# Order of the latent up projections and place of the modulation products in a two-block transformer kernel

## The chip, the cores and the metric

One Trainium2 chip (trn2), one core of it. The metric is the device time of one execution in microseconds (us). The kernel before was run three times: median 2625.8 us, from 2625.59 to 2627.35. One further execution was taken with the hardware profiler; all rows below are from that one.

## The reference, cut to what matters

Two blocks of two layers each run on a sequence of 512 tokens with 1024 features, all in float32. The change is in the first block only, in its token mixer, once per layer:

```python
mod = jax.nn.silu(c) @ w_ada[l] + b_ada[l]                 # 6 x 1024, the modulation
sh1, sc1, g1, sh2, sc2, g2 = jnp.split(mod[:, None, :], 6, axis=-1)
h = x * (1.0 + sc1) + sh1
proj = h @ w_in                                            # qa ka va iq ik iw cq ckv kr ga gb
...
# index scores of the sparse attention: sum over 8 heads of relu(iq . ik) * iw, top 128 kept
q  = (rms_norm(cq, q_norm_g) @ w_uq).reshape(bsz, seq, 8, 64 + 32)    # latent up, queries
q_nope, q_rope = q[..., :64], apply_rope(q[..., 64:], positions)
kv = (rms_norm(ckv, kv_norm_g) @ w_ukv).reshape(bsz, seq, 8, 64 + 64) # latent up, keys and values
```

Both versions compute all of it. The modulation of layer l is needed late: sh1 and sc1 first, g1 and part of sc2/sh2 by the end of the layer.

## The kernel before, in words

The program is written engine by engine with explicit semaphores; nothing schedules it. Each engine's list is in order, and a wait holds everything behind it on that engine.

**Weights.** Every weight slot is 128 x 2048 float32 (the slot of the key/value up projection, UKV, is 128 x 1024). SyncE loads it to w_raw (two buffers, L436), ScalarE rounds it to w_hi (`split_hi`, L1212), GpSimd forms w_lo = w_raw - w_hi (L550), and TensorE computes each product as three matmuls of 512 columns, hi x hi, lo x hi and hi x lo (`mm3`, L623 to L625). The slots of a layer follow each other: 0 to 3 the input projection for the index heads and latents, 4 to 7 the gate ga, 8 the query up projection (UQ), 9 UKV, 10 and 11 the first ones of the dense queries and keys (QK).

**Modulation.** Each layer's w_ada arrives in halves of 512 outputs, each as two loads (ring `ada_mid`, L430; a load waits until the one two before it is consumed). VectorE multiplies and adds it up in eight steps of 128 x 512, 4 per load: in a plain loop (`ada_halves`, L1686 and L1688), or one step at a time between other work (`ada_step_at`, L1702 and L1708). TensorE then sums over the partitions with matmuls of one column each (`ada_group`, L655); a float32 matmul is two passes, so 20 of them are 40 weight loads and 40 short matmuls. `ada_take` (L1714, L1717) adds the bias.

**The stretch of the change, per layer.** While TensorE runs the input projection, VectorE works through halves 4, 5 and 6 of the layer in the loop, and behind them in its list forms iw_tok (L1942), for which TensorE waits before the index scores. Index scores: 12 pairs of heads and query blocks (`PAIRS`); per pair TensorE has two score products (L867), then 5 or 6 of the 64 gate steps; ScalarE takes the relu (L1386), VectorE adds up (L1956, L1959). The banks of a pair are free again when VectorE has added up the pair two before. Between them stand two reciprocals of the latent norms (L1968, L1971) and 16 modulation steps of halves 7 and 8.

Latent up stage: 8 query tiles of 6 matmuls (two k-steps), then 4 key tiles of 3, then 4 value tiles of 3, through banks 0 to 3 in turn; after query tile 3 stand all 20 one-column products, in bank 7. For a query tile VectorE makes two rope products (L1989, L1990), then ScalarE copies the rest and frees the bank (L1409) and GpSimd adds the two (L586); VectorE writes the products of head h only after GpSimd has added those of head h-2. For a key tile ScalarE copies both heads (L1415, L1416). Value tiles are copied by VectorE (L1997), in order and after all key tiles are free. ScalarE splits slot 10 between the query tiles and the key tiles, and slot 11 after the last value tile. Then `attention(l, 1)` begins: TensorE's score product (L730) and three gate-like steps of slot 10 per unit beside it, which need w_lo of slot 10 and the bank of value tile 2.

## Time and profile before

| | before |
|---|---|
| median of 3 runs | 2625.8 us (2625.59 to 2627.35) |
| the profiled execution's own time | 2619.64 us |
| its span (first to last instruction) | 2617.9 us |
| time around the span | 1.7 us |
| TensorE busy | 2454.3 us, 94% |
| VectorE, ScalarE, GpSimd busy | 1195.2, 1022.6, 960.6 us |
| mean granted TensorE clock | 0.968 of full |
| index scores and up stage, layer 0 | about 99 to 191 us of the span |
| the same, layer 1 | about 954 to 1042 us |

In the timeline a row is: start, duration, engine, line, operation, out<-in, count, and in brackets the idle time before it with what ended it. PEld is TensorE's weight load, PE its matmul. Busy PE is not PE at its peak: a matmul of 512 columns is shown as 0.39 us long, though the next starts after 0.23 us. In the windows, PEclk is the granted clock as a share of the full 2.4 GHz.

### The profile page before, as it was taken

What the parts mean: (1) busy time and instruction counts of PE and PEld (TensorE: products, weight loads), DVE (VectorE), ACT (ScalarE), POOL (GpSimd) and SP (SyncE); (2) the same over time, 40 slices, a digit from 0 to 9 for tenths busy, and PEclk for the clock granted to TensorE, in tenths of its full rate; (3) what the DMA queues carried; (4) which work ended last, traced back from release to release, by engine and by line L of the source; (5) the groups of instructions that cost most, each with busy time, mean ns of one, the idle gap of its engine ahead of it and who ended that gap; (6) DMA issues with size and microseconds to landing.
All of it is one profiled execution on the core that took longest, in us unless ns stands there. A gap on an engine that the chain in (4) does not pass through costs nothing.

```text
span 2617.9 us, 32182 instructions
## 1 busy us (share of the span) xinstructions
PE 2454.3 (94%) x11316; PEld 1906.0 (73%) x11316; DVE 1195.2 (46%) x2581; ACT 1022.6 (39%) x1679; POOL 960.6 (37%) x780
## 2 busy tenths in 40 slices
PE   7999999899999899999989999989999989899877
PEld 4668767688888776876767888857788767577555
DVE  7555665654453465566555444134200530544562
ACT  6344344244442244434424444132223432323652
POOL 2342223434444434222344444443444434244211
PEclk9999999999999899999999999999999999899878
DMA  9521133222235342113322222222222202122100
GB/s 342 198 91 65 62 97 143 101 81 96 96 133 182 119 173 102 65 62 97 135 110 80 96 96 87 100 81 83 85 96 96 86 33 80 49 93 84 49 1 33
DMA packets 51985, 259.12 MB, mean 99 GB/s; under 512 B 6368, under 2 KB 16352, under 8 KB 26272
## 3 DMA queue, kind: packets, MB, share of 16 engines
q1 hardware_dynamic: 50720, 249.24, 27.4%
q0 software_dynamic: 1152, 8.39, 0.8%
q8 instruction: 69, 1.13, 0.2%
q14 instruction: 44, 0.36, 0.0%
HBM read 249.08 MB, written 7.34 MB: 98 GB/s over the span
## 4 chain that ended last, share of the span: by engine, by line
PE 87%; DVE 6%; ACT 3%; issue 3%; POOL 1%; DMA 1%; SPq 0%; DVEq 0%; ACTq 0%; POOLq 0%
PE bank L623 24%; PE bank L625 23%; PE bank L624 23%; PE bank L730 3%; PE bank L754 2%; PE bank L743 1%; PE bank L1069 1%; PE bank L998 1%; PE bank L1142 1%; PE bank L867 1%; PE bank L1161 1%; PE bank L655 1%; POOL w_lo L550 1%; PE bank L1058 1%; ACT w_hi L1212 1%
## 5 line engine op out<-in xcount | busy, mean ns | idle before, releaser
L550 POOL TENSOR_TENSOR w_lo<-w_raw,w_hi 128x512 fp32r<-128x512 f32 (+1 forms) x700 | 887.5, 1299 | 1444.1 <-ACT w_hi L1212 898.7
L623 PE MATMUL bank<-h_hi,w_hi 128*128 128x512 f32 x1792 | 735.8, 411 | 33.3 <-DVE h_lo L2083 14.3
L625 PE MATMUL bank<-h_hi,w_lo 128*128 128x512 f32 x1792 | 705.1, 393 | 0.0
L624 PE MATMUL bank<-h_lo,w_hi 128*128 128x512 f32 x1792 | 704.0, 393 | 0.0
L623 PEld LDWEIGHTS bank<-h_hi,w_hi 128*128 128x128 f32 x1792 | 341.0, 190 | 130.4 <-issue 62.2
L624 PEld LDWEIGHTS bank<-h_lo,w_hi 128*128 128x128 f32 x1792 | 341.0, 190 | 73.0 <-issue 8.4
L625 PEld LDWEIGHTS bank<-h_hi,w_lo 128*128 128x128 f32 x1792 | 339.6, 190 | 73.7
L1212 ACT ACTIVATE w_hi<-w_raw 128x2048 fp32r<-128x2048 f32 (+1 forms) x108 | 189.8, 1757 | 282.6 <-PE bank L625 243.8
L2041 DVE SCALAR_TENSOR_TENSOR cv<-bank,par,cv 128x511 f32<-128x511 f32 (+1 forms) x176 | 131.7, 749 | 215.2 <-ACT cv L1464 202.3
L1464 ACT ACTIVATE cv<-bank,par 128x512 f32<-128x512 f32 x88 | 68.3, 779 | 234.9 <-PE bank L625 234.9
L1217 ACT ACTIVATE w_hi<-w_raw 128x2048 fp32r<-128x2048 f32 x76 | 145.0, 1909 | 35.9 <-PE bank L625 35.9
L1288 ACT ACTIVATE L<-L,nmax 128x128 f32<-128x128 f32 (+3 forms) x128 | 72.0, 563 | 186.9 <-DVE nmax L1769 186.4
L623 PE MATMUL bank<-u_hi,w_hi 128*128 128x512 f32 x352 | 138.7, 394 | 0.0
L625 PE MATMUL bank<-u_hi,w_lo 128*128 128x512 f32 x352 | 137.7, 391 | 0.0
L624 PE MATMUL bank<-u_lo,w_hi 128*128 128x512 f32 x352 | 137.6, 391 | 0.0
L623 PE MATMUL bank<-w_hi,h_hi 128*128 128x512 f32 x256 | 100.8, 394 | 0.0
L625 PE MATMUL bank<-w_hi,h_lo 128*128 128x512 f32 x256 | 99.7, 389 | 0.0
L624 PE MATMUL bank<-w_lo,h_hi 128*128 128x512 f32 x256 | 99.6, 389 | 0.0
L1850 DVE SCALAR_TENSOR_TENSOR x<-bank,mod,x 128x512 f32<-128x512 f32 x32 | 24.0, 751 | 159.6 <-PE bank L625 158.6
L2121 DVE TENSOR_TENSOR wt<-bank,decay 128x512 f32<-128x512 f32 (+3 forms) x32 | 13.5, 484 | 172.0 <-PE bank L1058 171.8
L2092 DVE TENSOR_TENSOR rt<-bank,rope 128x512 f32<-128x512 f32 x32 | 22.1, 691 | 126.7 <-PE bank L998 112.5
L624 PEld LDWEIGHTS bank<-u_lo,w_hi 128*128 128x128 f32 x352 | 66.5, 189 | 14.3 <-issue 0.5
(345 smaller groups left out, 3669.3 us busy)
## 6 DMA issues: line engine op xcount, KB each, us to landing
w_raw<-w_stream SPq DMA_DIRECT2D x150, 1024.0 KB, 4.8
w_raw<-w_down SPq DMA_DIRECT2D x32, 704.0 KB, 4.1
ada_mid<-w_ada SPq DMA_DIRECT2D x20, 1024.0 KB, 6.9
ada_last<-w_ada SPq DMA_DIRECT2D x12, 1024.0 KB, 4.8
ada_early<-w_ada POOLq DMA_DIRECT2D x8, 1024.0 KB, 19.5
ada_late<-w_ada SPq DMA_DIRECT2D x8, 1024.0 KB, 6.2
bias_in<-bias_scratch SPq DMA_DIRECT2D x16, 256.0 KB, 3.1
bias_in<-bias_scratch SPq DMA_DIRECT2D x16, 192.0 KB, 2.7
```

The lines of the kernel that those rows point to most:

```text
L550: ins = nc.gpsimd.tensor_tensor(w_lo[r][:, part], w_raw[r][:, part], w_hi[r][:, part].bitcast(fp32), ALU.subtract)
L623: nc.tensor.matmul(out, w[0][:, cols], xh, start=first, stop=False)
L624: nc.tensor.matmul(out, w[0][:, cols], xl, start=False, stop=False)
L625: return nc.tensor.matmul(out, w[1][:, cols], xh, start=False, stop=last)
L655: ins = nc.tensor.matmul(banks[bank][:, j:j + 1], ada_acc[late][:, part + j // 4, (j % 4) * P:(j % 4 + 1) * P], ones[:, 0:1], start=True, ...
L730: nc.tensor.matmul(banks[4 + t % 2][:, 0:n], q[rows, hh, i * P:(i + 1) * P], kk[rows, hh, 0:n], start=True, stop=True).then_inc(s_done, 1)
L754: ins = nc.tensor.matmul(banks[u % 2][:, 0:HD], PT[u % 2][:, b * P:(b + 1) * P], v[:, b, h * HD:(h + 1) * HD], start=(b == 0), stop=(b == i))
L1212: A_(w_hi[n % 2][:, 0:cols], w_raw[n % 2][:, 0:cols], ACT.Copy).then_inc(w_hi_done, 1)
L1217: A_(w_hi[n % 2][:, :], w_raw[n % 2][:, :], ACT.Copy).then_inc(w_hi_done, 1)
L1288: A_(L[t % 3][:, 0:n], L[t % 3][:, 0:n], ACT.Exp, bias=nmax[:, t:t + 1], scale=-1.0, accum_out=esum[:, t:t + 1]).then_inc(exp_done, 1)
L1464: A_(cv[s][c][:, :], banks[(t + c) % 4][:, :], ACT.Identity, bias=b, scale=w2).then_inc(conv_first, 1)
L2041: return V.scalar_tensor_tensor(out, banks[(t + c) % 4][:, 0:S - 2 + w], weight, out, ALU.mult, ALU.add)
```

## The change

A table `UPS` puts the key tiles between the query tiles: q0 q1 q2 k0 q3 q4 k1 q5 q6 k2 q7 k3, on TensorE and ScalarE alike; VectorE keeps its order of heads. The 20 one-column products are issued in twos, after each of the tiles at positions 4 to 11 and after value tiles 0 and 1. The modulation half 6 leaves the loop ahead of iw_tok and joins halves 7 and 8 inside the index scores, two steps per pair. The wait of pair 1 for the loop, and the place of `ada_take`, move with it.

```diff
--- before.py
+++ after.py
@@ -411,6 +411,8 @@
         def ended(kind, u):
             return next((t for t, k in BESIDE[kind][u] if k == BESIDE_LAST[kind]), None) if 0 <= u < len(BESIDE[kind]) else None
 
+        UPS = [("q", 0), ("q", 1), ("q", 2), ("k", 0), ("q", 3), ("q", 4), ("k", 1), ("q", 5), ("q", 6), ("k", 2), ("q", 7),
+               ("k", 3)]
         LOADS = 16 * 3
         BIAS_UNITS = [(i, 8 * i + q) for i in range(NB) for q in range(8)]
         BIAS_BANKS = (2, 3, 6, 7)
@@ -648,6 +650,12 @@
                         if after_slot:
                             after_slot(it, s)
 
+            def ada_columns_at(first, count):
+                for j in range(first, first + count):
+                    ins = nc.tensor.matmul(banks[7][:, j:j + 1], ada_acc[0][:, j // 4, (j % 4) * P:(j % 4 + 1) * P],
+                                           ones[:, 0:1], start=True, stop=True)
+                return ins
+
             def ada_group(first, halves, late, bank):
                 pe.wait_ge(ada_used, 2 * (first + halves))
                 part = first % 12 - 4 if first % 12 else 0
@@ -861,7 +869,7 @@
                     if u >= 2:
                         pe.wait_ge(idx_acc, NI * l + 2 * (u - 1))
                     if u == 1:
-                        pe.wait_ge(ada_used, 2 * (12 * l + 7))
+                        pe.wait_ge(ada_used, 2 * (12 * l + 6))
                     for c in range(2):
                         rows = slice(c * HD, (c + 1) * HD)
                         nc.tensor.matmul(banks[4 + 2 * (u % 2) + c][:, 0:n], iq[rows, p, i * P:(i + 1) * P], ik2[rows, 0:n],
@@ -883,24 +891,28 @@
 
                 pe.wait_ge(c_done, 3 * (l + 1))
                 w = split(l, SLOT_UQ)
+                wkv = split(l, SLOT_UKV)
                 wait_slot(l, SLOT_UQ)
-                for h in range(H):
-                    wait_bank(l, TILE_UQ + h, 2 if h < 2 else 4)
-                    if h == 3:
+                for pos, (what, j) in enumerate(UPS):
+                    wait_bank(l, TILE_UQ + pos, 2 if pos < 2 else 4)
+                    if pos == 3:
                         pe.wait_ge(ada_used, 2 * (12 * l + 9))
-                    tile(banks[h % 4][:, :], w, h * 2 * P, c_hi, c_lo, 2).then_inc(tile_done, 1)
-                    if h == 3:
                         pe.wait_ge(idx_acc, NI * (l + 1))
-                        ada_group(12 * l + 4, 5, 0, 7)
-                w = split(l, SLOT_UKV)
-                wait_slot(l, SLOT_UKV)
-                for j in range(4):
-                    wait_bank(l, TILE_UK + j)
-                    tile(banks[j][:, :], w, j * P, c_hi, c_lo, 1, 2).then_inc(tile_done, 1)
+                        wait_slot(l, SLOT_UKV)
+                    if what == "q":
+                        tile(banks[pos % 4][:, :], w, j * 2 * P, c_hi, c_lo, 2).then_inc(tile_done, 1)
+                    else:
+                        tile(banks[pos % 4][:, :], wkv, j * P, c_hi, c_lo, 1, 2).then_inc(tile_done, 1)
+                    if pos >= 4:
+                        ada_columns_at(2 * pos - 8, 2)
                 for m in range(NB):
                     wait_bank(l, TILE_UV + m)
                     mm3(banks[m][:, :], (c_hi[:, 2, m * P:(m + 1) * P], c_lo[:, 2, m * P:(m + 1) * P]), slice(0, P),
-                        w[0][:, 512:1024], w[1][:, 512:1024], True, True).then_inc(tile_done, 1)
+                        wkv[0][:, 512:1024], wkv[1][:, 512:1024], True, True).then_inc(tile_done, 1)
+                    if m < 2:
+                        ins = ada_columns_at(16 + 2 * m, 2)
+                        if m:
+                            ins.then_inc(ada_sum, 1)
                 attention(l, 1)
 
                 A = aidx(l, 1)
@@ -1403,17 +1415,20 @@
                         m = SLOT_GA + tt // 2 + 2
                         split_hi(l, m, 1024 if m == SLOT_UKV else SLOT)
 
-                for h in range(H):
-                    act.wait_ge(tile_done, tdone(l, TILE_UQ + h))
-                    act.wait_ge(q_rope, H * l + h + 1)
-                    A_(qm[0:64, h, :], banks[h % 4][0:64, :], ACT.Copy).then_inc(tile_evac, 1)
-                split_hi(l, SLOT_UQ + 2)
-                act.wait_ge(ada_used, 2 * (12 * l + 9))
                 act.wait_ge(kr_turned, l + 1)
-                for j in range(4):
-                    act.wait_ge(tile_done, tdone(l, TILE_UK + j))
-                    A_(km[0:64, 2 * j, :], banks[j][0:64, :], ACT.Copy)
-                    A_(km[0:64, 2 * j + 1, :], banks[j][64:128, :], ACT.Copy).then_inc(tile_evac, 1)
+                for pos, (what, j) in enumerate(UPS):
+                    b = banks[pos % 4]
+                    act.wait_ge(tile_done, tdone(l, TILE_UQ + pos))
+                    if what == "q":
+                        act.wait_ge(q_rope, H * l + j + 1)
+                        A_(qm[0:64, j, :], b[0:64, :], ACT.Copy).then_inc(tile_evac, 1)
+                        if j == H - 1:
+                            split_hi(l, SLOT_UQ + 2)
+                    else:
+                        if j == 0:
+                            act.wait_ge(ada_used, 2 * (12 * l + 9))
+                        A_(km[0:64, 2 * j, :], b[0:64, :], ACT.Copy)
+                        A_(km[0:64, 2 * j + 1, :], b[64:128, :], ACT.Copy).then_inc(tile_evac, 1)
                 act.wait_ge(tile_done, tdone(l, TILE_UV + 3))
                 split_hi(l, SLOT_UKV + 2)
                 softmax(l, 1)
@@ -1937,7 +1952,7 @@
                     dve.wait_ge(rope_ready, 1)
                     chain(V.tensor_scalar(rope[64:128, S:2 * S], rope[64:128, S:2 * S], ck[64:128, C_SGN:C_SGN + 1], None,
                                           ALU.mult))
-                ada_halves(12 * l + 5, 2, 0, 1, 7)
+                ada_halves(12 * l + 5, 1, 0, 1, 7)
                 dve.wait_ge(iw_done, l + 1)
                 V.tensor_scalar(iw_tok[:, :], banks[4][:, 0:32], H ** -0.5, None, ALU.mult).then_inc(iw_ready, 1)
                 dve.wait_ge(iw_ready, l + 1)
@@ -1978,23 +1993,24 @@
                             dve.wait_ge(c_hid, 3 * l + j + 1)
                             V.tensor_tensor(c_lo[:, j, :], c_raw[:, j, :], f32(c_hi[:, j, :]), ALU.subtract
                                             ).then_inc(c_done, 1)
-                    for e in range(16 * u // len(PAIRS), 16 * (u + 1) // len(PAIRS)):
-                        ada_step_at(12 * l + 7 + e // 8, 3 + e // 8, e % 8 // 4, e % 4)
+                    for e in range(2 * u, 2 * u + 2):
+                        ada_step_at(12 * l + 6 + e // 8, 2 + e // 8, e % 8 // 4, e % 4)
                 dve.wait_ge(idx_acc, NI * (l + 1))
 
                 for h in range(H):
-                    dve.wait_ge(tile_done, tdone(l, TILE_UQ + h))
+                    pos = UPS.index(("q", h))
+                    b = banks[pos % 4]
+                    dve.wait_ge(tile_done, tdone(l, TILE_UQ + pos))
                     if h >= 2:
                         dve.wait_ge(q_sum, H * l + h - 1)
-                    V.tensor_tensor(q_cos[h % 2][64:96, :], banks[h % 4][64:96, :], rope[64:96, 0:S], ALU.mult)
-                    V.tensor_tensor(q_sin[h % 2][64:96, :], banks[h % 4][96:128, :], rope[96:128, S:2 * S], ALU.mult
+                    V.tensor_tensor(q_cos[h % 2][64:96, :], b[64:96, :], rope[64:96, 0:S], ALU.mult)
+                    V.tensor_tensor(q_sin[h % 2][64:96, :], b[96:128, :], rope[96:128, S:2 * S], ALU.mult
                                     ).then_inc(q_rope, 1)
-                    if h == 5:
-                        ada_take(l, 1)
                 for m in range(NB):
                     dve.wait_ge(tile_done, tdone(l, TILE_UV + m))
                     dve.wait_ge(tile_evac, tdone(l, TILE_UV + m - 1))
                     V.tensor_copy(vm[:, m, :], banks[m][:, :]).then_inc(tile_evac, 1)
+                ada_take(l, 1)
                 softmax(l, 1)
                 topk_loop(2, TOPK // 8 + 1 - AHEAD)
                 topk_step(2, TOPK // 8)
```

On TensorE, in the up stage of layer 0 (c_hi and c_lo are the normed latents, w_hi_52 is the UQ slot, w_hi_53 the UKV slot, ada_acc_early the summed modulation), before:

```order
L623 MATMUL bank<-c_hi,w_hi_52 128x512
L624 MATMUL bank<-c_lo,w_hi_52 128x512
L625 MATMUL bank<-c_hi,w_lo_54 128x512
L655 MATMUL bank<-ck,ada_acc_early 128x1 x20
L623 MATMUL bank<-c_hi,w_hi_52 128x512
```

and now, from the middle of it:

```order
L655 MATMUL bank<-ck,ada_acc_early 128x1 x2
L625 MATMUL bank<-c_hi,w_hi_53 128x512
L626 MATMUL bank<-c_lo,w_hi_53 128x512
L627 MATMUL bank<-c_hi,w_lo_55 128x512
L655 MATMUL bank<-ck,ada_acc_early 128x1 x2
L625 MATMUL bank<-c_hi,w_hi_52 128x512
```

The block of 20 has become ten groups of two, and a key tile (w_hi_53) stands between query tiles.

On ScalarE, in the same stage (qm and km are the query and key outputs; w_hi_52<-w_raw_50 is the split of slot 10, the last row that of slot 11), before:

```order
L1212 ACTIVATE w_hi_53<-w_raw_51 128x1024
L1409 ACTIVATE qm<-bank 64x512 x8
L1212 ACTIVATE w_hi_52<-w_raw_50 128x2048
L1415 ACTIVATE km<-bank 64x512
L1416 ACTIVATE km<-bank 64x512
...
L1212 ACTIVATE w_hi_53<-w_raw_51 128x2048
```

and now:

```order
L1224 ACTIVATE w_hi_53<-w_raw_51 128x1024
L1424 ACTIVATE qm<-bank 64x512 x3
L1430 ACTIVATE km<-bank 64x512
L1431 ACTIVATE km<-bank 64x512
L1424 ACTIVATE qm<-bank 64x512 x2
...
L1424 ACTIVATE qm<-bank 64x512
L1224 ACTIVATE w_hi_52<-w_raw_50 128x2048
L1430 ACTIVATE km<-bank 64x512
L1431 ACTIVATE km<-bank 64x512
L1224 ACTIVATE w_hi_53<-w_raw_51 128x2048
```

Three of the four key tiles are now copied ahead of the split of slot 10, which still follows the last query tile.

On VectorE, from the loop into the index scores of layer 0, now (before, the loop ran three times in all, and the 16 steps were spread one or two to a pair):

```order
L1703 SCALAR_TENSOR_TENSOR bank<-ada_mid_144,csilu,bank 128x512 x3
L1703 SCALAR_TENSOR_TENSOR ada_acc_early<-ada_mid_144,csilu,bank 128x512
L1692 REGISTER_ALU
L1692 COMPARE_AND_BRANCH
L1957 TENSOR_SCALAR iw_tok<-bank 128x32
L1971 TENSOR_SCALAR sel<-bank,iw_tok 128x256
L1974 SCALAR_TENSOR_TENSOR sel<-bank,iw_tok,sel 128x256
L1717 TENSOR_SCALAR bank<-ada_mid_143,csilu 128x512
L1723 SCALAR_TENSOR_TENSOR bank<-ada_mid_143,csilu,bank 128x512
L1974 SCALAR_TENSOR_TENSOR sel<-bank,iw_tok,sel 128x256 x2
```

iw_tok now follows one pass of the loop, and every pair is followed by two steps.

## Rows read from the trace of the kernel before

**Rows 1.** The page: the span, and the engines of the chain that ended last.
```profile
span 2617.9 us, 32182 instructions
...
PE 87%; DVE 6%; ACT 3%; issue 3%; POOL 1%; DMA 1%; SPq 0%; DVEq 0%; ACTq 0%; POOLq 0%
```

**Rows 2.** Timeline, layer 0, from the input projection into the index scores.
```profile
88.11 0.33 SPq L430 DMA_DIRECT2D ada_mid<-w_ada  x1
...
95.74 2.34 DVE L1688 SCALAR_TENSOR_TENSOR bank<-ada_mid,csilu,bank 128x512 f32<-128x512 f32 x3 [2.79 <-DMA ada_mid<-w_ada]
...
96.01 0.39 PE L625 MATMUL bank<-h_hi,w_lo 128*128 128x512 f32 x1
...
99.46 0.33 PEld L867 LDWEIGHTS bank<-ik,iq 64*128 64x128 f32 x4 [3.48 <-issue]
...
102.01 0.63 PE L625 MATMUL bank<-h_hi,w_lo 128*128 128x512 f32 x1
...
107.05 0.30 PEld L867 LDWEIGHTS bank<-ik,iq 64*128 64x128 f32 x4 [0.76 <-issue]
```

**Rows 3.** Timeline, layer 1, the same place: pairs 0 and 1.
```profile
953.54 0.33 PEld L867 LDWEIGHTS bank<-ik,iq 64*128 64x128 f32 x4 [1.83 <-issue]
...
959.59 0.30 PEld L867 LDWEIGHTS bank<-ik,iq 64*128 64x128 f32 x4 [0.76 <-issue]
```

**Rows 4.** Timeline, layer 0, pairs 5 and 6, and VectorE's dearest work between.
```profile
125.86 0.30 PEld L867 LDWEIGHTS bank<-ik,iq 64*128 64x128 f32 x4 [0.35 <-issue]
...
128.57 3.34 DVE L1971 RECIPROCAL c_sq<-c_sq 128x512 f32<-128x512 f32 x1
...
131.02 0.30 PEld L867 LDWEIGHTS bank<-ik,iq 64*128 64x128 f32 x4 [0.35 <-issue]
...
133.94 0.75 DVE L1708 SCALAR_TENSOR_TENSOR bank<-ada_mid,csilu,bank 128x512 f32<-128x512 f32 x1
```

**Rows 5.** Timeline, layer 0, the latent up stage.
```profile
159.84 0.19 PEld L623 LDWEIGHTS bank<-c_hi,w_hi 128*128 128x128 f32 x1
...
161.70 0.69 DVE L1989 TENSOR_TENSOR L<-bank,rope 32x512 f32<-32x512 f32 x1 [2.09 <-PE bank L625]
...
161.89 2.54 POOL L550 TENSOR_TENSOR w_lo<-w_raw,w_hi 128x512 fp32r<-128x512 f32 x2 [6.45 <-ACT w_hi L1212]
...
165.28 5.56 PEld L655 LDWEIGHTS bank<-ck,ada_acc_early 128*128 128x128 f32 x40
...
170.73 0.33 PEld L623 LDWEIGHTS bank<-c_hi,w_hi 128*128 128x128 f32 x1
...
181.86 0.59 ACT L1409 ACTIVATE qm<-bank 64x512 f32<-64x512 f32 x1 [0.84 <-DVE O L1990]
...
182.35 1.90 ACT L1212 ACTIVATE w_hi<-w_raw 128x2048 fp32r<-128x2048 f32 x1
...
184.33 4.97 POOL L550 TENSOR_TENSOR w_lo<-w_raw,w_hi 128x512 fp32r<-128x512 f32 x4 [1.22 <-ACT w_hi L1212]
...
189.11 3.08 DVE L1997 COPY vm<-bank 128x512 f32<-128x512 f32 x4 [7.34 <-ACT km L1416]
...
191.50 0.19 PEld L623 LDWEIGHTS bank<-h_hi,w_hi 128*128 128x128 f32 x1 [1.25 <-issue]
```

**Rows 6.** Timeline, layer 1, start, one-column products and end of that stage.
```profile
1012.38 0.19 PEld L623 LDWEIGHTS bank<-c_hi,w_hi 128*128 128x128 f32 x1
...
1017.82 4.84 PEld L655 LDWEIGHTS bank<-ck,ada_acc_early 128*128 128x128 f32 x40
...
1022.54 0.34 PEld L623 LDWEIGHTS bank<-c_hi,w_hi 128*128 128x128 f32 x1
...
1042.45 0.19 PEld L623 LDWEIGHTS bank<-h_hi,w_hi 128*128 128x128 f32 x1 [1.45 <-issue]
```

**Rows 7.** Windows: stretch, length, busy and count per engine, PEclk, DMA share, GB/s.
```profile
165.30:170.70 5.40, 5.40 (x42) 5.36 (x40) 2.77 (x4) 1.18 (x2) 4.23 (x4) 0.83 0.65 207
170.70:177.00 6.30, 6.30 (x19) 5.03 (x19) 2.25 (x4) 0.59 (x1) 1.27 (x1) 0.60 0.00 0
```

## The prediction, made before the changed kernel ran

> **What bounds the kernel.** The first view is the chain of waits: 87% of the span is TensorE's own work [rows 1], so time is won where TensorE waits or runs slow. The second view is the timeline of the two places that the diff touches, read backwards from the row at which TensorE goes on; the third is the granted clock by window. They show three losses in each layer.
>
> First, before the index scores. TensorE's last matmul of the input projection starts at 96.01, and the first score product loads at 99.46, after 3.48 us without a load. In between VectorE ends the modulation loop (the load issued at 88.11 is first used at 95.74, and four steps follow), and iw_tok stands behind it [rows 2]. In layer 1 the gap is 1.83 [rows 3]. A score product with nothing to wait for has a gap of 0.35 [rows 4], so 3.13 and 1.48 us are the loop's.
>
> Second, the clock behind that gap. In layer 0 a matmul at 102.01 lasts 0.63 instead of 0.39 us: 1.2 GHz. Pair 0 to pair 1 takes 107.05 - 99.46 = 7.59 us [rows 2], and in layer 1, at 2.4 GHz, 959.59 - 953.54 = 6.05 [rows 3]. A fall of the clock so costs 1.54 us.
>
> Third, the up stage. It lasts from 159.84 to 191.50, 31.66 us [rows 5], and from 1012.38 to 1042.45, 30.07 us [rows 6], counted to the load of the first step beside the attention. TensorE has far less to do in it: 72 matmuls at 0.227 (24 take 165.28 - 159.84 = 5.44) and 40 short passes. The 40 take 1022.54 - 1017.82 = 4.72 us in layer 1, 0.118 each [rows 6], and 5.45 in layer 0 [rows 5]; together 21.1 us. The rest is low clock after the block of one-column products (0.60 of full over 6.3 us [rows 7], a loss of 2.5 us), and a tail in which TensorE waits for ScalarE: slot 10 is split at 182.35 for 1.90 us, only then are eight key halves copied at 0.6 us each, and VectorE's value copies begin at 189.11 [rows 5].
>
> **Part 1, the moved modulation half.** Eight steps of 0.75 us [rows 4] leave the loop; with one half less it ends near 88.1, since the row of its next load, issued when half 5 is consumed, stands there [rows 2]. iw_tok is then some ten us early, and TensorE goes on at 96.33: minus 3.13 and minus 1.48. Without the gap the clock has no reason to fall in layer 0: minus 1.54. The eight steps, 6.2 us with their gaps, now stand among the pairs. Pair 5 takes TensorE 131.02 - 125.86 = 5.2 us, and it is VectorE's worst: the reciprocal of 3.34, two steps of 0.75, and two additions and three products that are each no longer than a step [rows 4], some 8.3 us. It falls behind by some 3 us and catches up over pairs 6 and 7; TensorE waits only for the additions of the pair two before, which leaves about 3 us to spare. I cost it at nothing; if that cover were gone, each us of lag beyond it is a us of TensorE. SyncE: the loads of half 7 now wait for half 6 inside the pairs, and the weight loads of slots 7 to 9 queue behind them. By my count slot 7 is issued at 109 instead of 104 and split at about 128; the modulation load issued with it is needed 11 us later and the slowest seen took 95.74 - 88.11 = 7.6 us [rows 2]. Nothing is late.
>
> **Part 2, the up stage.** Time t runs from the stage's first load; everything before it is shifted as a whole.
> - q0 to q2 end at 4.08. k0 needs w_lo of UKV, whose row ends 161.89 + 2.54 = t 4.59 [rows 5]: a new wait of 0.5 us, k0 ends at 5.33.
> - From there to the end of q7 stand five query tiles (6.80), two key tiles (1.36) and six pairs of columns, 24 passes x 0.118 = 2.83: t = 16.3. The ScalarE and VectorE work of each tile is by then 2 us or more ahead of the bank's next use, since the key copies (1.2 us) fit between query copies (0.59).
> - After q7: 0.50 to VectorE's start (its first row is at t 1.86, the tile ends at 1.36), two products 1.4, ScalarE's copy 0.1 + 0.59: t = 18.9. Split of slot 10, 1.90: 20.8. GpSimd's four parts, 4.97 + 0.1: t = 25.9 [rows 5].
> - k3 is copied after the split, to 22.1, value tile 3 ends at 22.8, the value copies at 25.2. So the **low half of slot 10 is what is late next**: TensorE goes on at t = 26.0. `ada_take` (two small operations) falls before that, and the first transposes stand two units behind it.
>
> The stage then takes 26.0: minus 5.66 in layer 0, minus 4.07 in layer 1. But TensorE is idle from about t 23 to 26. A gap of that length in [rows 2] cost 1.54, and I charge that at the head of the attention in both layers: plus 3.08.
>
> Bounds. How a pair of one-column products prices between wide matmuls is not in these rows. Nearest below: its first load hides, three passes of 0.118; above: one load of 0.19 more is exposed. Over the six pairs on the path that is -0.7 to +1.1 us a layer; I take 0.118 a pass as in the block, because there the loads already paced it. The charge for the clock lies between 0 and 1.54 per layer.
>
> The Trainium skill, "TensorE: Matmul & The Clock Gate", section "Loop structure matters more than you think", has it that matmuls issued back to back keep the engine warm and that a wait between bursts is when the "PE goes cold". The trace disagrees in one place: the clock was 0.83 over 165.3 to 170.7 and 0.60 after it, while the engine was busy 5.40 of 5.40 us [rows 7]; one-column passes alone took it down. By that section the spread columns could not harm the clock and rivals C and E have no chance (2613.0 stands); by the row they could, and 2619.4 is open.
>
> **Sum.** Layer 0: 3.13 + 1.54 + 5.66 - 1.54 = 8.79. Layer 1: 1.48 + 4.07 - 1.54 = 4.01. Together **12.8 us**: span 2617.9 to 2605.1, that execution's 2619.6 to 2606.8. The runs' median stands 6.2 us above the profiled execution, so 2625.8 - 12.8 = **2613.0**. Behind the stage TensorE is busy nearly without a break, so the gain should reach the end.
>
> **Rivals.**
> - **B, the clock holds at the head of the attention** in both layers. For: in layer 1 an idle gap of 1.83 us cost no clock [rows 3]. Against: [rows 2]. Saves 15.9 us: 2609.9. Chance 0.20.
> - **C, the spread columns still bring the clock down once a layer.** For: [rows 7], left after their block. Against: wide matmuls now hold over 60% of the time between. Price as in layer 0 before, 2.5 plus the block's 5.45 - 4.72 = 0.7: 3.2 a layer, 6.4: 2619.4. Chance 0.10.
> - **D, the index scores give the first part back.** VectorE's lag at pair 5, or a modulation load stuck behind a weight slot, makes TensorE wait by 3 to 6 us; or iw_tok was not the last wait, and the change does not do there what it says. For: 8.3 us of work against 5.2. Against: the slack worked out above. At worst the whole 6.15 is lost: 2619.2. Chance 0.09.
> - **E, slower.** The clock falls at position 4 of the up stage and stays at 1.2 GHz until the attention, since each pair of columns comes before it has recovered. The 11.0 us of work from t 5.3 to 16.3 then take twice that, which puts t at 37: plus 5.3 and 6.9, plus 3.1 at the head of the attention, minus 6.1 of part 1: **9 us slower, 2635**. It decides against the change once the low clock covers some 60% of those 11 us in both layers. For: [rows 7]. Against: there the passes stood alone; with six matmuls of 512 columns between, nothing in the rows shows it. Chance 0.04.
> - The forecast keeps 0.57.
>
> **How the numbers follow.** The likeliest case gives 2613.0, with its own range of 2611 to 2616 by the bounds of the columns and half the clock's charge. The range reaches down to B with cheap columns (2609.9 - 1.4 = 2608.5) and up to C and D with dear ones (2620.5); E and the tails are left out. A measurement can tell 0.2%, 5.25 us, from no change. Forecast, B, C and most of D lie beyond it (C and D by a us only, so part of them, 0.06, counts as the same); slower is E, 0.04; faster is 0.90.
>
> **What would show it.** In the changed profile: the load of the first score product at about 96.3 with a gap near 0.35, and at 952.1 in layer 1; clock 1.00 over pair 0; the stage's first load at about 155.2 and 1010.9; k0 waiting for GpSimd's w_lo by half a us; ten groups of x4 short passes at 0.47 us each with wide matmuls at 0.39 between them; the split of slot 10 ended at t 20.8, and the first load beside the attention at t 26.0, released by GpSimd. The prediction is wrong if that load comes after t 28, if a score product waits for `sel`, or if matmuls of 0.63 us appear between the pairs of columns.

## The result, and the profile after

| | before | after |
|---|---|---|
| median of 4 runs | 2625.70 us (2623.18 to 2627.35) | 2609.24 us (2603.87 to 2609.83) |
| ratio, with 95% interval | | 0.9934 [0.9916, 0.9951] |
| the profiled execution | 2619.64 us | 2609.83 us |
| its span | 2617.9 us | 2608.0 us |
| TensorE busy | 2454.3 us | 2452.2 us |
| mean granted clock | 0.968 | 0.968 |

The changed kernel is faster. By the ratio the gain is 0.0066 x 2625.8 = 17 us, with an interval from 13 to 22. By the spans of the two profiled executions it is 9.9 us. The prediction said 12.8 and lies between these two. That one change has two sizes is the main question of the experiments. The two profiles themselves give part of the answer: at the places of the change they differ by 13.7 us (first and sixth row of the table below), and 3.8 us of that is lost elsewhere, 0.9 of it ahead of the first of these places, where the last projection matmul starts at 96.91 instead of 96.01.

The diff adds lines ahead of most helpers, so the old L623 to L625 are L625 to L627 in what follows, the score product's L867 is L875, the attention's L730 is L738, the copies L1409, L1415 and L1416 are L1424, L1430 and L1431, the split L1212 is L1224, GpSimd's L550 is L552. Timeline of after, layer 0, where the index scores begin (beside [rows 2]); a row is start, duration, engine, line, operation, count, and in brackets the idle time and what ended it:

```profile
88.03 0.75 DVE L1703 SCALAR_TENSOR_TENSOR ada_acc_early<-ada_mid,csilu,bank 128x512 f32<-128x512 f32 x1
88.98 0.19 DVE L1957 TENSOR_SCALAR iw_tok<-bank 128x32 f32<-128x32 f32 x1 [0.20 <-DVE ada_acc_early L1703]
...
96.91 0.39 PE L627 MATMUL bank<-h_hi,w_lo 128*128 128x512 f32 x1
97.22 0.30 PEld L875 LDWEIGHTS bank<-ik,iq 64*128 64x128 f32 x4 [0.35 <-issue]
...
103.22 0.30 PEld L875 LDWEIGHTS bank<-ik,iq 64*128 64x128 f32 x4 [0.76 <-issue]
```

VectorE's loop now starts its last step at 88.03, and iw_tok stands at 88.98, eight us before the last projection matmul at 96.91. The gap of 3.48 us is 0.35, and pair 0 to pair 1 is 103.22 - 97.22 = 6.00 us instead of 7.59. Layer 1 has 0.35 and 951.53 - 945.54 = 5.99:

```profile
945.54 0.30 PEld L875 LDWEIGHTS bank<-ik,iq 64*128 64x128 f32 x4 [0.35 <-issue]
951.53 0.30 PEld L875 LDWEIGHTS bank<-ik,iq 64*128 64x128 f32 x4 [0.76 <-issue]
```

The moved steps cost the index scores nothing. Timeline of after, layer 0, round the reciprocal (beside [rows 4]):

```profile
122.02 0.30 PEld L875 LDWEIGHTS bank<-ik,iq 64*128 64x128 f32 x4 [0.35 <-issue]
...
124.74 3.34 DVE L1986 RECIPROCAL c_sq<-c_sq 128x512 f32<-128x512 f32 x1
...
127.19 0.30 PEld L875 LDWEIGHTS bank<-ik,iq 64*128 64x128 f32 x4 [0.35 <-issue]
...
130.11 1.54 DVE L1723 SCALAR_TENSOR_TENSOR bank<-ada_mid,csilu,bank 128x512 f32<-128x512 f32 x2
...
131.68 0.30 PEld L875 LDWEIGHTS bank<-ik,iq 64*128 64x128 f32 x4 [0.35 <-issue]
```

Pair 5's two steps end at 131.65, when pair 7 is about to start (131.68), and still each score load has a gap of 0.35: the lag stays under the slack.

Timeline of after, layer 0, the up stage (beside [rows 5]):

```profile
156.01 0.19 PEld L625 LDWEIGHTS bank<-c_hi,w_hi 128*128 128x128 f32 x1
...
160.71 0.19 PEld L625 LDWEIGHTS bank<-c_hi,w_hi 128*128 128x128 f32 x1 [0.66 <-issue]
...
162.67 0.64 PEld L655 LDWEIGHTS bank<-ck,ada_acc_early 128*128 128x128 f32 x4
163.23 0.19 PEld L625 LDWEIGHTS bank<-c_hi,w_hi 128*128 128x128 f32 x1
...
174.69 1.90 ACT L1224 ACTIVATE w_hi<-w_raw 128x2048 fp32r<-128x2048 f32 x1
...
176.67 9.90 POOL L552 TENSOR_TENSOR w_lo<-w_raw,w_hi 128x512 fp32r<-128x512 f32 x8 [1.21 <-ACT w_hi L1224]
...
177.73 0.19 PEld L625 LDWEIGHTS bank<-w_hi,c_hi 128*128 128x128 f32 x1 [0.92 <-ACT km L1431]
177.78 3.07 DVE L2012 COPY vm<-bank 128x512 f32<-128x512 f32 x4 [3.67 <-ACT km L1431]
...
181.68 0.19 PEld L625 LDWEIGHTS bank<-h_hi,w_hi 128*128 128x128 f32 x1 [2.96 <-POOL w_lo L552]
...
187.86 0.14 PEld L751 LDWEIGHTS bank<-ck,L 128*128 128x128 f32 x1
```

The stage takes 181.68 - 156.01 = 25.67 us, and in layer 1 the same 25.67 (next rows). Ten groups of four short passes stand between the tiles, and 162.67 to 163.23 is 0.56, less the 0.12 by which the next load follows closer: about 0.45 a group over all, or 0.11 a pass, where the block had 0.118. The split of slot 10 starts 18.7 us into the stage, its low half is ready 25.6 us into it, and TensorE waits 2.96 us for it. Layer 1:

```profile
1004.32 0.19 PEld L625 LDWEIGHTS bank<-c_hi,w_hi 128*128 128x128 f32 x1
...
1026.04 0.19 PEld L625 LDWEIGHTS bank<-w_hi,c_hi 128*128 128x128 f32 x1 [0.92 <-ACT km L1431]
...
1029.99 0.29 PEld L625 LDWEIGHTS bank<-h_hi,w_hi 128*128 128x128 f32 x1 [2.95 <-POOL w_lo L552]
```

Windows of after over the columns and tiles, and over the wait with the head of the attention in layer 1 (columns as in [rows 7]):

```profile
165.30:170.70 5.40, 5.40 (x31) 4.62 (x31) 3.36 (x6) 2.80 (x5) 3.50 (x3) 1.00 0.03 14
170.70:177.00 6.30, 6.30 (x39) 5.41 (x37) 1.80 (x3) 4.47 (x6) 2.89 (x3) 1.00 0.00 0
1028.00:1034.60 6.60, 4.61 (x15) 3.77 (x16) 2.67 (x9) 3.07 (x6) 6.60 (x6) 0.74 0.44 159
```

With the columns spread the clock holds (1.00 against 0.83 and 0.60). It falls behind the wait for GpSimd instead: from the first load beside the attention to the first transposes is 6.18 us in layer 0, 187.86 - 181.68, where before it was 4.56.

### The profile page after: what moved, and what is told of

Read it like the earlier page. It is cut to its first block, busy times and chain, and to the rows that moved or that the text cites. A ratio compares the mean times of both kernels' runs of the same rounds, so it can differ in the third digit from the quotient of the medians.

```text
span 2608.0 us, 32138 instructions
## 1 busy us (share of the span) xinstructions
PE 2452.2 (94%) x11316; PEld 1904.3 (73%) x11316; DVE 1193.8 (46%) x2581; ACT 1021.8 (39%) x1679; POOL 960.4 (37%) x780
## 4 chain that ended last, share of the span: by engine, by line
PE 87%; DVE 5%; ACT 3%; issue 2%; POOL 2%; DMA 1%; SPq 0%; DVEq 0%; POOLq 0%; ACTq 0%
PE bank L625 24%; PE bank L627 24%; PE bank L626 23%; PE bank L738 3%; PE bank L762 2%; PE bank L751 1%; POOL w_lo L552 1%; PE bank L1081 1%; PE bank L1010 1%; PE bank L1154 1%; PE bank L875 1%; PE bank L1173 1%; PE bank L1070 1%; PE bank L786 1%; ACT w_hi L1224 0%
## 5 line engine op out<-in xcount | busy, mean ns | idle before, releaser
L552 POOL TENSOR_TENSOR w_lo<-w_raw,w_hi 128x512 fp32r<-128x512 f32 (+1 forms) x700 | 887.3, 1299 | 1439.9 <-ACT w_hi L1224 892.6
L625 PE MATMUL bank<-h_hi,w_hi 128*128 128x512 f32 x1792 | 736.9, 411 | 36.6 <-DVE h_lo L2099 14.3
L627 PE MATMUL bank<-h_hi,w_lo 128*128 128x512 f32 x1792 | 706.1, 394 | 0.0
L625 PEld LDWEIGHTS bank<-h_hi,w_hi 128*128 128x128 f32 x1792 | 341.6, 191 | 134.2 <-issue 59.5
L627 PEld LDWEIGHTS bank<-h_hi,w_lo 128*128 128x128 f32 x1792 | 340.2, 190 | 73.7
L1224 ACT ACTIVATE w_hi<-w_raw 128x2048 fp32r<-128x2048 f32 (+1 forms) x108 | 189.8, 1757 | 281.5 <-PE bank L627 242.4
L625 PE MATMUL bank<-u_hi,w_hi 128*128 128x512 f32 x352 | 138.8, 394 | 0.0
L627 PE MATMUL bank<-u_hi,w_lo 128*128 128x512 f32 x352 | 137.6, 391 | 0.0
L625 PE MATMUL bank<-w_hi,h_hi 128*128 128x512 f32 x256 | 100.8, 394 | 0.0
L627 PE MATMUL bank<-w_hi,h_lo 128*128 128x512 f32 x256 | 99.7, 389 | 0.0
```

Of the source, the lines that this page charges most:

```text
L552: ins = nc.gpsimd.tensor_tensor(w_lo[r][:, part], w_raw[r][:, part], w_hi[r][:, part].bitcast(fp32), ALU.subtract)
L625: nc.tensor.matmul(out, w[0][:, cols], xh, start=first, stop=False)
L627: return nc.tensor.matmul(out, w[1][:, cols], xh, start=False, stop=last)
L1224: A_(w_hi[n % 2][:, 0:cols], w_raw[n % 2][:, 0:cols], ACT.Copy).then_inc(w_hi_done, 1)
```

## The experiments

Five lengths in each layer's trace are compared, and the span: the **gap** from the last projection load to the first score load (0.54 where nothing waits), **pair 0 to 1** (5.99 to 6.04 at full clock), the **index scores** to the stage's first load (58.8, or 60.4 with a fall of the clock in pair 0; not in the table), the **up stage**, and the **head**, from the first load beside the attention to the first transposes (4.56 at full clock). In us, layer 0 / layer 1:

| kernel | gap | pair 0 to 1 | up stage | head | span |
|---|---|---|---|---|---|
| before | 3.67 / 2.02 | 7.59 / 6.04 | 31.66 / 30.06 | 4.56 / 4.57 | 2617.9 |
| e1 before | 3.62 / 1.75 | 7.61 / 6.02 | 31.68 / 32.98 | 4.60 / 4.55 | 2620.8 |
| e9 before | 3.54 / 2.00 | 7.59 / 6.02 | 31.67 / 30.06 | 4.60 / 4.55 | 2620.1 |
| e10 before | 3.36 / 2.38 | 7.62 / 6.00 | 31.64 / 31.39 | 4.59 / 4.57 | 2622.5 |
| e11 before | 3.37 / 2.19 | 7.61 / 7.60 | 31.70 / 31.64 | 4.57 / 4.57 | 2623.6 |
| after | 0.54 / 0.54 | 5.99 / 5.99 | 25.67 / 25.67 | 6.19 / 5.91 | 2608.0 |
| e5 after | 0.54 / 0.54 | 5.99 / 5.99 | 25.67 / 25.68 | 6.16 / 6.17 | 2602.5 |
| e12 after | 0.54 / 0.54 | 5.99 / 5.99 | 25.66 / 25.66 | 6.18 / 7.44 | 2606.9 |
| e2 half moved | 0.54 / 0.54 | 5.99 / 5.99 | 31.64 / 31.68 | 4.59 / 4.57 | 2615.5 |
| e3 up stage | 3.49 / 1.88 | 7.58 / 6.00 | 25.66 / 25.68 | 5.92 / 6.18 | 2610.4 |
| e4 block | 0.54 / 0.54 | 5.99 / 5.99 | 30.53 / 28.96 | 5.93 / 5.96 | 2615.9 |
| e6 late columns | 0.54 / 0.54 | 5.99 / 5.99 | 23.36 / 23.35 | 4.55 / 4.58 | 2599.6 |
| e7 early split | 0.54 / 0.54 | 5.99 / 5.99 | 24.70 / 24.70 | 4.57 / 6.17 | 2602.8 |
| e8 both | 0.54 / 0.54 | 5.99 / 5.99 | 22.47 / 22.46 | 4.55 / 4.58 | 2599.6 |

### e1: the kernel before, once more

No edit.

> The kernel before, unchanged, once more, for its trace and its spread. Theory M (the change is worth what the two traces show at its own places, about 12 us, and executions differ by falls of the clock elsewhere): the ratio is 1.000, the trace puts the up stage at 31.7 and 30.1 us as in the first profile, and its span lies anywhere between 2616 and 2626, the difference explained by matmuls of 0.63 us at other places. Theory S (the typical execution of the kernel before loses more at the places of the change than the profiled one did, so that the change is worth 16 us): a profile with a span near 2624 shows extra low clock in the gap before the index scores of layer 1 or in the up stages.

Measured: 2622.63 us (2620.49 to 2627.75, 11 runs), ratio 1.0001 [0.9992, 1.0009]; the kernel before on the same chip 2622.96 (2619.24 to 2627.54, 23 runs). The profile differs from the first in one term of the sum: layer 1's up stage takes 32.98 us, not 30.06. So the 2625.8 from which the prediction subtracts is the upper part of a spread of 8 us, and the profile below it had a short stage.

### e2: the modulation half moved, alone

The changed lines of part 1, put into the kernel before:

```diff
-                        pe.wait_ge(ada_used, 2 * (12 * l + 7))
+                        pe.wait_ge(ada_used, 2 * (12 * l + 6))
-                ada_halves(12 * l + 5, 2, 0, 1, 7)
+                ada_halves(12 * l + 5, 1, 0, 1, 7)
-                    for e in range(16 * u // len(PAIRS), 16 * (u + 1) // len(PAIRS)):
-                        ada_step_at(12 * l + 7 + e // 8, 3 + e // 8, e % 8 // 4, e % 4)
+                    for e in range(2 * u, 2 * u + 2):
+                        ada_step_at(12 * l + 6 + e // 8, 2 + e // 8, e % 8 // 4, e % 4)
```

> The kernel before with the modulation half moved into the index scores alone (the up stage stays as it was). Theory M: the first score product loads 0.35 us after the input projection in both layers, no low clock over pair 0; 6.1 us faster (ratio 0.9977), no wait for sel in the index scores. Rival D (VectorE's lag gives it back): 0 to 3 us faster, and score products wait for sel. Theory S allows up to 9 us, if layer 1 too used to lose the clock there.

Measured: 2616.78 us (2615.24 to 2618.13, 7 runs), ratio 0.9976 [0.9965, 0.9986], 6.3 us. Part 1 of the sum is 3.13 + 1.54 + 1.48 = 6.15. Both gaps are 0.54, pair 0 to 1 is 5.99 in both layers, and the index scores take 58.79 us in both.

### e3: the up stage, alone

The same three edits the other way round, in the changed kernel.

> The changed kernel with the modulation half back in the loop ahead of iw_tok, so that the up stage is changed alone. Theory M: up stage 25.7 us instead of 31.7 and 30.1, a fall of the clock at the head of the attention in both layers, 6 to 7 us faster (ratio 0.9975); this and the half alone add up to the whole change. Theory S: 8 to 10 us faster.

Measured: 2614.52 us (2610.01 to 2618.43, 8 runs), ratio 0.9968 [0.9957, 0.9979], 8.4 us (5.5 to 11.3, which excludes neither theory). Part 2 of the sum is 5.66 + 4.07 - 3.08 = 6.65. The gaps are back (3.49 and 1.88), and the stage is 25.66 and 25.68. The two parts add up: 6.3 + 8.4 = 14.7.

### e4: the new order, but the columns in one block

```diff
-                    if pos >= 4:
-                        ada_columns_at(2 * pos - 8, 2)
+                    if pos == 4:
+                        ada_group(12 * l + 4, 5, 0, 7)
...
-                    if m < 2:
-                        ins = ada_columns_at(16 + 2 * m, 2)
-                        if m:
-                            ins.then_inc(ada_sum, 1)
```

> The changed kernel with all 20 one-column products in one block again, after query tile 3, the order of tiles and the moved half kept. Theory M (my prediction: spreading keeps the clock up, the passes themselves cost the same 4.7 us): the clock falls to 1.2 GHz behind the block as in the kernel before, so that the end of q7 comes 1.2 to 2.5 us later, less what the passes now behind q7 took from the path (four pairs, 1.9 us, now lie before it): up stage 27 to 30 us, the kernel 3 to 8 us slower than the changed one, ratio to before 0.995 to 0.997. Rival (the spreading is worth nothing, it is the order of tiles that counts): the stage is 27.6 us by the four pairs alone and the ratio within 0.001 of 0.9945.

Measured: 2616.5 us (2611.94 to 2620.42, 7 runs), ratio 0.9975 [0.9963, 0.9986]; the changed kernel had 0.9934 to 0.9948. The stage takes 30.53 and 28.96 us, 4.9 and 3.3 more than with the columns spread, though the passes are the same 40. Windows of e4, layer 0 (columns as in [rows 7]), and the block in both layers in the timeline:

```profile
160.00:165.00 5.00, 4.74 (x26) 3.76 (x24) 3.55 (x6) 1.34 (x3) 4.59 (x5) 1.00 0.52 118
165.00:171.00 6.00, 6.00 (x35) 5.88 (x36) 1.16 (x2) 2.09 (x4) 2.33 (x2) 0.66 0.32 135
171.00:176.00 5.00, 5.00 (x18) 3.93 (x17) 1.90 (x3) 1.48 (x3) 1.28 (x1) 0.73 0.00 0
```

```profile
163.94 6.19 PEld L663 LDWEIGHTS bank<-ck,ada_acc_early 128*128 128x128 f32 x40
...
1015.39 4.67 PEld L663 LDWEIGHTS bank<-ck,ada_acc_early 128*128 128x128 f32 x40
```

The clock falls while TensorE is busy without a break, and the changed kernel, with the same wait for k0 ahead of its columns, keeps it, so it is the block that takes it down. Not all of the 4.9 and 3.3 us is clock: in e4 all 40 passes stand ahead of q7, in the changed kernel 24, and the other 16 are 1.9 us at 0.118 each. The low clock is the remaining 3.0 and 1.4 us. Spreading the columns, with the place of the last ones behind q7, is thus most of the second part's gain: by the ratio e4 keeps 6.6 us, and about 6 of them are part 1's.

### e5: the change again, beside e6 to e8

> The changed kernel, unchanged, once more. By the first four runs the kernel before spreads from 2619.2 to 2627.5 (median 2623.0 of 23), and the two parts alone gave 6.2 and 8.4 us. Theory M (16.5 us was read between a high sample of before and a fair one of the change; the parts add): 14.6 us, ratio 0.9944, within 0.001. Theory S (the change is worth 16.5 us): ratio 0.9934 or less again. In the trace: up stage 25.7 us in both layers, score product 0.35 us after the projection.

Measured: 2607.95 us (2604.3 to 2611.88, 6 runs), ratio 0.9942 [0.9928, 0.9957]; the kernel before on that chip 2625.5 (2616.88 to 2627.54, 11 runs). Theory M's 0.9944 is the nearer one; theory S's 0.9934 is not excluded by this run alone. The span of the profile is 5.5 us below that of the first profile of the same kernel, with every length of the table but one within 0.03 us. The difference lies outside the change. Windows of after and of e5, the same stretch of layer 0 far behind the diff:

```profile
448.00:455.00 7.00, 5.54 (x18) 4.48 (x19) 1.13 (x2) 4.29 (x5) 4.12 (x4) 0.76 0.31 131
```

```profile
448.00:455.00 7.00, 6.58 (x29) 5.51 (x30) 0.16 (x1) 3.25 (x3) 5.03 (x4) 1.00 0.21 89
```

One execution has a fall of the clock there, the other none. Of stretches with three or more matmuls at 1.2 GHz behind 60 us, the five profiles of the kernel before have 16, 15, 15, 18 and 16; the three of the changed one 13, 11 and 14.

### e6: the columns behind the last query tile, in fours

```diff
-                    if pos >= 4:
-                        ada_columns_at(2 * pos - 8, 2)
+                    if pos >= 10:
+                        ada_columns_at(4 * pos - 40, 4)
...
-                    if m < 2:
-                        ins = ada_columns_at(16 + 2 * m, 2)
-                        if m:
+                    if m < 3:
+                        ins = ada_columns_at(8 + 4 * m, 4)
+                        if m == 2:
```

> The changed kernel with no one-column products before query tile 7 ends: four each after q7, k3 and value tiles 0 to 2. Theory M (the path to the first step beside the attention is TensorE to q7, then rope, copy, split and low half of slot 10): the 2.8 us of six pairs leave the path; then VectorE's rope products set q7, and the stage takes 22.3 to 22.7 us instead of 25.7, the idle time at its end goes, and with it the fall of the clock at the head of the attention: 6 to 9 us faster than the changed kernel. Rival (four products, eight passes, per three wide matmuls are enough to bring the clock down): matmuls of 0.63 us between the groups, the stage 24 us or more, under 5 us faster.

Measured: 2601.51 us (2595.94 to 2603.63, 6 runs), ratio 0.9912 [0.9896, 0.9927]; no run of it is as slow as the fastest of e5. Timeline of e6, layer 0:

```profile
163.20 0.19 PEld L625 LDWEIGHTS bank<-c_hi,w_hi 128*128 128x128 f32 x1 [0.21 <-ACT qm L1424]
...
164.29 0.19 PEld L625 LDWEIGHTS bank<-c_hi,w_hi 128*128 128x128 f32 x1 [0.55 <-ACT km L1431]
...
168.96 1.08 PEld L655 LDWEIGHTS bank<-ck,ada_acc_early 128*128 128x128 f32 x8
...
171.37 1.90 ACT L1224 ACTIVATE w_hi<-w_raw 128x2048 fp32r<-128x2048 f32 x1
...
173.34 4.98 POOL L552 TENSOR_TENSOR w_lo<-w_raw,w_hi 128x512 fp32r<-128x512 f32 x4 [1.21 <-ACT w_hi L1224]
...
178.37 0.19 PEld L625 LDWEIGHTS bank<-h_hi,w_hi 128*128 128x128 f32 x1 [1.05 <-POOL w_lo L552]
```

The columns now fill TensorE's wait for the low half instead of standing ahead of q7. Of the 2.83 us of passes taken off the path, 2.3 arrive: without them the tiles catch up with the copies, and TensorE waits 0.21 and 0.55 us for banks. Five groups of eight passes between tiles do not lower the clock either. Windows of e6:

```profile
155.00:168.96 13.96, 13.57 (x59) 10.47 (x58) 9.69 (x14) 7.31 (x13) 10.26 (x9) 1.00 0.38 114
168.96:176.90 7.94, 7.94 (x57) 7.28 (x56) 3.46 (x5) 5.08 (x7) 6.02 (x5) 1.00 0.00 0
176.90:183.00 6.10, 5.24 (x26) 4.27 (x25) 2.34 (x8) 4.19 (x6) 5.10 (x5) 1.00 0.48 172
```

And with the wait cut to 1.05 us the clock holds at the head of the attention as well (last row, and 4.55 and 4.58 us to the transposes). Against e5 the trace gives 2.31 + 2.33 + 1.61 + 1.59 = 7.8 us at these places, the two ratios 0.0030 x 2625.8 = 7.9 (with an interval of about 2 to 13), the two medians 6.4.

### e7: slot 10 split before the last query copy

```diff
                     if what == "q":
+                        if j == H - 1:
+                            split_hi(l, SLOT_UQ + 2)
                         act.wait_ge(q_rope, H * l + j + 1)
                         A_(qm[0:64, j, :], b[0:64, :], ACT.Copy).then_inc(tile_evac, 1)
-                        if j == H - 1:
-                            split_hi(l, SLOT_UQ + 2)
```

> The changed kernel, but ScalarE splits slot 10 as soon as query tile 7 is done on TensorE, ahead of its copy instead of behind it. Theory M (the low half of slot 10 is the last wait of the stage): the split starts 1.8 us earlier and the stage takes 23.9 instead of 25.7 us in both layers: 3.6 us faster, a little more where the shorter idle time saves the clock. Rival (value copies or the key tile behind the split set the end): 25 us or more, no gain, since copies of q7 and k3 now come later.

Measured: 2605.01 us (2602.76 to 2611.82, 6 runs), ratio 0.9934 [0.9918, 0.9950]. Timeline of e7, layer 0:

```profile
173.96 1.90 ACT L1224 ACTIVATE w_hi<-w_raw 128x2048 fp32r<-128x2048 f32 x1
```

```profile
175.35 1.27 POOL L588 TENSOR_TENSOR qm<-PT,O 32x512 f32<-32x512 f32 x1 [1.70 <-DVE O L2007]
176.85 6.22 POOL L552 TENSOR_TENSOR w_lo<-w_raw,w_hi 128x512 fp32r<-128x512 f32 x5 [0.23 <-POOL qm L588]
```

The stage is 0.97 us shorter in both layers, where 1.8 was expected: the split ends at 175.86, but GpSimd is at the rotation of q7 until 176.62 and starts its parts at 176.85. By the time alone this is not told from e5. Its head is a small experiment of its own: the wait is 2.75 us in both layers, and the clock fell in layer 1 (6.17) and not in layer 0 (4.57).

### e8: e6 and e7 together

> Both edits: columns behind query tile 7 and the split ahead of its copy. Theory M: slot 10's low half is ready at about t 21.1, and TensorE's own work (72 matmuls, 40 passes and the wait for k0, 21.6 us) becomes the bound: stage 21.7 to 22.2 us, no idle time at its end, no fall of the clock at the head of the attention: 9 to 11 us faster than the changed kernel, ratio to before about 0.990. Rival as for the columns alone: the clock falls within the stage, 24 us.

Measured: 2601.34 us (2595.79 to 2604.7, 6 runs), ratio 0.9912 [0.9896, 0.9928]. The stage is 0.9 us a layer below e6's, at 22.47 us a little over the 21.7 to 22.2 expected, and the time is the same; against e5 it is 7.9 us by the ratios, not 9 to 11. The two profiles differ in falls of the clock elsewhere: e8's has low stretches at 76 and from 1289 us which e6's lacks, and e6's has some at 445 and 1328 us which e8's lacks. So the equal spans do not tell whether the 1.8 us are there on the average, and six runs do not either. e6 and e8 are both faster than the changed kernel.

### e9, e10, e11: the kernel before, three more profiles

No edit.

> The kernel before, for a third profile (with e10 and e11). Theory R (the up stage of layer 1 in the first profile, 30.06 us, was a lucky execution, and the term of 4.07 us that the prediction took from it was too small): layer 1 shows 31.6 to 33.0 us here, as the 31.64 and 31.68 of the stages in e2 and the 32.98 in e1, and layer 0 shows 31.7. Theory S (the 30.06 is usual and e1's 32.98 was the exception): 30.0 to 30.2 in layer 1 in at least two of e9, e10 and e11, and the change's 16.5 us then stay unexplained by that term.

> As e9: theory R 31.6 to 33.0 us for the up stage of layer 1, theory S 30.0 to 30.2. The number of falls of the clock outside the changed stages should differ from e9's by one or two, 1.5 us each.

> As e9: theory R 31.6 to 33.0 us for the up stage of layer 1, theory S 30.0 to 30.2. Mean of the five profiles of this kernel for layer 1: by R 31.4 to 32.4, so that the term of the sum becomes 5.8 to 6.7 us instead of 4.07 (before the charge for the clock it was 30.07 minus 26.0).

Measured: one time each, 2621.84, 2624.29 and 2625.34 us. Neither theory holds as stated. Layer 1's stage is 30.06, 31.39 and 31.64: the 30.06 is neither the exception nor the rule, since it came in two of five executions. The mean of five is (30.06 + 32.98 + 30.06 + 31.39 + 31.64) / 5 = 31.23, just under the range given for R. The block itself takes 6.70, 4.66, 5.11 and 5.40 us in e1, e9, e10 and e11 (beside the 4.84 of [rows 6]), from 0.2 less to 1.9 us more, where the stages differ by up to 2.9; the rest is low clock behind it. Windows of 15 us from 7.5 us into the stage of layer 1, in the order before, e1, e9, e10, e11 (columns as in [rows 7]):

```profile
1019.90:1034.90 15.00, 13.16 (x60) 10.27 (x60) 8.20 (x12) 5.04 (x7) 7.63 (x6) 0.89 0.13 55
```

```profile
1021.50:1036.50 15.00, 14.40 (x55) 12.12 (x54) 7.47 (x12) 2.94 (x5) 5.70 (x5) 0.66 0.12 51
```

```profile
1021.00:1036.00 15.00, 13.19 (x60) 10.13 (x59) 8.17 (x12) 5.05 (x7) 7.58 (x6) 0.89 0.12 50
```

```profile
1024.60:1039.60 15.00, 13.93 (x59) 11.14 (x58) 8.22 (x12) 3.70 (x7) 7.10 (x6) 0.77 0.13 54
```

```profile
1022.80:1037.80 15.00, 13.79 (x57) 11.07 (x57) 8.20 (x12) 3.47 (x7) 6.86 (x6) 0.77 0.13 54
```

PEclk is the last figure but two. A mean of 0.89 over 15 us is 2 x 0.11 x 15 = 3.3 us at half clock (1.2 GHz); TensorE so spent about 3.3, 10.2, 3.3, 6.9 and 6.9 us there, and the stages are 30.06, 32.98, 30.06, 31.39 and 31.64. The same 40 passes cost more or less by how long the clock stays low in and behind them, and that differs between executions, also on one chip: e9, e10 and e11 ran on the same one. In e11 the clock also fell in layer 1's pair 0 (7.60 us), as it had only in layer 0 so far. The window from the gap through that pair, e11:

```profile
953.00:960.60 7.60, 5.99 (x21) 4.34 (x20) 3.08 (x6) 4.49 (x7) 4.79 (x4) 0.78 0.39 164
```

### e12: the change, a third time

> The changed kernel, for a third profile and more timed rounds. Both theories: the up stage 25.67 us in both layers, the gap before the first score product 0.54, and between the first load beside the attention and the first transposes 5.9 to 6.2 us (the clock falls there) or 4.6 (it does not). Ratio to the kernel before: theory R, about 15 us of 2625: 0.9943; theory S, 12.8 us: 0.9951; a further unexplained gain of the change of 16.5 us: 0.9937. Only pooled with the two earlier comparisons can the first and the second be told apart, if at all.

Measured: 2608.98 us (2606.13 to 2611.97, 5 runs), ratio 0.9948 [0.9934, 0.9962], against 2623.82 (2620.09 to 2625.33, 9 runs). The mean of the three ratios of the changed kernel is (0.9934 + 0.9942 + 0.9948) / 3 = 0.9941, and their half widths together give 0.0009: 15.4 us, from 13 to 18. The stages and gaps are as expected; the head of layer 1 takes 7.44 us, more than the 5.9 to 6.2 of a single fall. The mean ratio is nearest to theory R's 0.9943. By this the gain is larger than the 12.8 us of the sum, by about 2.6.

## Why the prediction was wrong

The sum against the means of five profiles of before and three of after, in us saved:

| term | predicted, layer 0 / 1 | measured, layer 0 / 1 |
|---|---|---|
| gap before the index scores | 3.13 / 1.48 | 2.97 / 1.53 |
| clock in pair 0 | 1.54 / 0 | 1.61 / 0.35 |
| up stage | 5.66 / 4.07 | 6.00 / 5.56 |
| clock at the head of the attention | -1.54 / -1.54 | -1.59 / -1.94 |
| sum | 8.79 / 4.01 | 8.99 / 5.50 |

The mechanism was right at each place, and layer 0 is right to 0.2 us. **The step that failed is layer 1's term, "minus 4.07 in layer 1"**, and beside it the zero for the clock of its pair 0. Both were read from one execution, in which the clock was low for only about 3.3 us behind the block of columns and did not fall at all in pair 0. On the average of five the stage is 1.17 us longer than in that execution, which with 25.67 instead of 26.0 makes 5.56, and the fall in pair 0 costs 0.35. The sum becomes 14.5 instead of 12.8, and 14.7 are the measured gains of e2 and e3 together. Of the 15.4 measured the last us is not located; it is within the interval. The means of the spans differ by 2621.0 - 2605.8 = 15.2.

A second step is not in the sum but in the level: "the runs' median stands 6.2 us above the profiled execution, so 2625.8 - 12.8". The surplus was not something that stays with the kernel. Executions of before went from 2616.9 to 2627.75 us in 61 runs, the medians of three further comparisons were 2623.0, 2625.5 and 2623.8, and the profiled 2619.6 was simply one of the short ones. The range had no term for this; its lower end was rival B with cheap columns, a case that did not happen, while the first comparison, 17 us by its ratio, is the largest of the three.

Point by point:
- **The order of the stage.** k0's load comes 0.85 us after the one before it instead of 0.23, so the wait for w_lo costs 0.6 (half a us was foreseen), the split ends 20.6 us into the stage (20.8), and TensorE goes on after 25.67 (26.0), released by GpSimd. That the low half of slot 10 would be late next is right.
- **The price of the spread passes** is 0.11 each, within the bounds and close to the 0.118 taken.
- **The charge for the clock at the head** of 1.54 a layer is right in kind in eight of eight cases of this stage (after, e3, e5, e12), at 1.34 to 1.63, once 2.87. Rival B, given 0.20, did not come in the three profiles of this kernel.
- **Rival C** is refuted by the windows of after (1.00) and by e6 with groups of eight.
- **Rival D** is refuted by e2: the index scores take 58.79 us, and no score product waits for `sel`.
- **Rival E** is refuted with C. The Trainium skill ("TensorE: Matmul & The Clock Gate", section "Loop structure matters more than you think") has the clock suffer from waits between bursts. Its half on waits agrees with the table below; e4's windows (0.66 with TensorE busy 6.00 of 6.00 us) show that a block of one-column products lowers it with no wait in that window; there the trace disagrees with it.

What the prediction did not see is that the kernel before had a fall close by as well: in the tail of its up stage, after the waits for ScalarE, the clock was at half in both layers of all five profiles, and it was back only before the head of the attention. The window of before, layer 0, ahead of the 191.50 of [rows 5]:

```profile
186.00:189.30 3.30, 3.25 (x8) 1.96 (x7) 0.19 (x1) 2.93 (x5) 3.30 (x3) 0.50 0.00 0
```

Its price is inside the 31.66, so the sum is not touched; but the change did not bring a new fall, it moved one from inside the stage to behind it.

## What to carry to other kernels

Where a change removes a fall of the clock, one profile gives a sample of its price, not the price: profile the kernel several times, compare stage lengths, and give the range a term for the spread between executions of the same program. The one-column products cost more than their passes where all 20 stood in a block; between wide tiles, two to four at a time, they cost about 0.11 us a pass, and the clock held at 1.00. Put such filler where the engine waits anyway, not ahead of what the wait is for: here that was worth another 7.8 us by the trace, 3.2 of them the wait's own cost in clock.

## What the runs showed of the hardware that was not expected

How often the clock fell during a wait of TensorE or within 1.6 us behind it, at the places of the change, over all profiles (the wait is the idle time of the weight loads, as in the brackets of the rows):

| place | wait, us | clock fell |
|---|---|---|
| head of the attention, e6 and e8 | 0.14 to 1.06 | 0 of 4 |
| the same, before (5 profiles) and e2 | 0.9 to 1.5 | 0 of 12 |
| first score product, layer 1, before and e3 | 1.56 to 2.19 | 1 of 6 |
| tail of the up stage, before and e2 | 2.35 or 2.36, after two of 0.9 to 1.3 | 12 of 12 |
| tail of the up stage, e4, with the head behind it | 2.36, then 2.17 or 2.25 | 2 of 2 |
| head of the attention, e7 | 2.75 | 1 of 2 |
| the same, after, e3, e5, e12 | 2.95 or 2.96, after one of 0.92 | 8 of 8 |
| first score product, layer 0, before and e3 | 3.17 to 3.48 | 6 of 6 |

Between about 1.6 and 2.8 us the same wait at the same place costs 1.6 us in one execution and nothing in another; the length of the wait alone does not decide. With other waits shortly before it, one of 2.35 us was always followed by a fall. So a wait of this size has a price of its length plus a chance of 1.6 us, and the timed runs of an unchanged program spread by 0.4%. What makes the difference between two executions is left open: no run here controls it. One small thing beside: VectorE's last operation on the modulation, on 4 columns, took 0.56 us in the changed kernel, where GpSimd was in the middle of forming a part of w_lo, and 0.17 in e6, where it began 0.05 us before such a part ended. That the one waits for the other is not shown. The rows are of after, then of e6.

```profile
181.09 0.56 DVE L1732 TENSOR_SCALAR mod<-mod 128x4 f32<-128x4 f32 x1
```

```profile
178.27 0.17 DVE L1732 TENSOR_SCALAR mod<-mod 128x4 f32<-128x4 f32 x1
```
